# One product of 672 columns, cut along its rows, for the compressed queries, keys and rotary columns of the second mixer

## The reference

```python
def second_block(x, g_norm, w_in, ...):
    h = rms_norm(x, g_norm[l])
    proj = h @ w_in[l]
    hy_in, z_hy, c_q, c_kv, k_rope, z_attn, gate_hy, gate_attn = jnp.split(proj, split_at, axis=-1)
    ...
    q = (rms_norm(c_q, g_cq[l]) @ w_uq[l]).reshape(B, L, MLA_HEADS, QK_DIM)
    kv = (rms_norm(c_kv, g_ckv[l]) @ w_ukv[l]).reshape(B, L, MLA_HEADS, QK_NOPE + V_DIM)
    k_r = jnp.broadcast_to(k_rope[:, :, None, :], (B, L, MLA_HEADS, QK_ROPE))
```

## Time and profile before

| | |
|---|---|
| median of 3 runs | 1084.29 us (1083.72 to 1084.83) |
| the profiled execution, own time | 1085.98 us |
| its span, first to last instruction | 1084.2 us |
| TensorE (PE) busy, matmuls | 1078.1 us, 99% |
| weight loads (PEld) busy | 1020.2 us, 94% |
| VectorE (DVE) busy | 793.9 us, 73% |
| ScalarE (ACT) busy | 592.2 us, 55% |
| granted TensorE clock, mean | 1.000 |
| DMA mean | 176 GB/s |

### The profile page before, as it was taken

The page is one execution under the profiler, slowest core; times in us unless marked ns, Lnnn a source line. Parts: engine busy times, 40 slices in busy tenths (PEclk is TensorE's granted clock), DMA queues, the critical chain, the costliest instruction groups (busy, mean ns, idle before and its releaser), DMA issues.

```text
span 1084.2 us, 21114 instructions
## 1 busy us (share of the span) xinstructions
PE 1078.1 (99%) x8588; PEld 1020.2 (94%) x8588; DVE 793.9 (73%) x1117; ACT 592.2 (55%) x842; POOL 0.2 (0%) x4
## 2 busy tenths in 40 slices
PE   9999999999999999999999999999999999999999
PEld 7999999999989999999999998999999799999998
DVE  5665657989999877778778555775655887997784
ACT  5544444578643345878446546444444576655461
POOL 0000000000000000000000000000000000000000
PEclk9999999999999999999999999999999999999999
DMA  8765555455443454444656533465555356543341
GB/s 343 289 220 205 184 183 210 151 204 192 160 156 118 142 190 157 156 164 148 206 169 240 195 116 118 147 233 193 193 187 200 117 177 214 175 156 117 118 155 40
DMA packets 29170, 190.71 MB, mean 176 GB/s; under 512 B 3656, under 2 KB 4457, under 8 KB 7274
## 3 DMA queue, kind: packets, MB, share of 16 engines
q1 hardware_dynamic: 26480, 182.53, 48.2%
q10 hardware_dynamic: 2618, 7.14, 2.0%
HBM read 188.61 MB, written 1.05 MB: 175 GB/s over the span
## 4 chain that ended last, share of the span: by engine, by line
PE 96%; DVE 1%; DMA 1%; ACT 1%; issue 0%; SPq 0%; ACTq 0%; DVEq 0%
PE bank L525 16%; PE bank L526 16%; PE bank L527 16%; PE bank L537 11%; PE bank L538 11%; PE bank L539 11%; PE bank L624 3%; PE bank L760 1%; DMA sb_w_raw<-in_w 1%; PE bank L708 1%; PE bank L874 1%; PE bank L1022 1%; PE bank L1242 1%; PE bank L1034 1%; PE bank L1078 1%; PE bank L1100 1%
## 5 line engine op out<-in xcount | busy, mean ns | idle before, releaser
L2087 DVE TENSOR_TENSOR sb_w_lo<-sb_w_raw,sb_w_hi 128x2048 fp32r<-128x2048 f32 x169 | 386.4, 2289 | 129.6 <-ACT sb_w_hi L1370 128.9
L1370 ACT ACTIVATE sb_w_hi<-sb_w_raw 128x2048 fp32r<-128x2048 f32 x169 | 322.8, 1910 | 32.1 <-PE bank L527 27.9
L525 PE MATMUL bank<-sb_hT_hi,sb_w_hi 128*128 128x256 f32 (+1 forms) x816 | 226.0, 277 | 0.0
L527 PE MATMUL bank<-sb_hT_hi,sb_w_lo 128*128 128x256 f32 (+1 forms) x816 | 225.9, 277 | 0.0
L526 PE MATMUL bank<-sb_hT_lo,sb_w_hi 128*128 128x256 f32 (+1 forms) x816 | 225.8, 277 | 0.0
L537 PE MATMUL bank<-sb_hT_hi,sb_w_hi 128*128 128x256 f32 (+2 forms) x744 | 213.1, 286 | 0.0
L538 PE MATMUL bank<-sb_hT_lo,sb_w_hi 128*128 128x256 f32 (+2 forms) x744 | 206.4, 277 | 0.0
L539 PE MATMUL bank<-sb_hT_hi,sb_w_lo 128*128 128x256 f32 x744 | 206.1, 277 | 0.0
L525 PEld LDWEIGHTS bank<-sb_hT_hi,sb_w_hi 128*128 128x128 f32 (+1 forms) x816 | 152.8, 187 | 0.0
L526 PEld LDWEIGHTS bank<-sb_hT_lo,sb_w_hi 128*128 128x128 f32 (+1 forms) x816 | 152.7, 187 | 0.0
L527 PEld LDWEIGHTS bank<-sb_hT_hi,sb_w_lo 128*128 128x128 f32 (+1 forms) x816 | 152.7, 187 | 0.1
(11 more groups left out here) (513 smaller groups left out, 2092.7 us busy)
## 6 DMA issues: line engine op xcount, KB each, us to landing
sb_w_raw<-in_w SPq DMA_DIRECT2D x169, 1024.0 KB, 4.9
sb_w_raw<-in_w SPq DMA_DIRECT2D x4, 512.0 KB, 7.4
sb_hT<-in_xT SPq DMA_DIRECT2D x2, 512.0 KB, 5.3
sb_x<-in_x SPq DMA_DIRECT2D x2, 512.0 KB, 11.3
sb_mem_xn<-in_mem ACTq DMA_DIRECT2D x1, 1024.0 KB, 6.9
sb_mem_T<-in_memT ACTq DMA_DIRECT2D x1, 1024.0 KB, 10.4
sb_post_g<-in_ffn_post_g ACTq DMA_DIRECT2D x2, 512.0 KB, 5.8
sb_decay<-in_c_decay ACTq DMA_DIRECT2D x1, 768.0 KB, 5.4
```

The source lines that it names most:

```text
L525: pe.matmul(o, a_hi, b_hi, start=first, stop=False)
L527: return pe.matmul(o, a_lo, b_hi, start=False, stop=last)
L1370: act.activation(w_hi[b % STAGES][:], w_raw[b % RING][:], ACT.Copy).then_inc(w_hi_in, 1)
L2087: tt(w_lo[b % STAGES][:], w_raw[b % RING][:], f32(w_hi[b % STAGES][:]), ALU.subtract).then_inc(w_lo_in, 1)
```

## The change

The three blocks of c are cut in another way. Before, each held all 1024 rows and some of the columns: 256, 256 and 160. Now each holds all 672 columns and some of the rows: tiles k 0 to 2, 3 to 5, and 6 and 7 (`C_PARTS`). One block is used for 2 halves of the tokens and 2 halves of the columns, 336 each, so that four banks (0, 1, 2 and 7) are open at once and stay open over all three blocks; they can be read only when block 141 has been used. ScalarE therefore reads c after all three, in 8 instructions where there were 8 of other widths, and no longer between the roundings of blocks 142 and 143. `norm_turn(6)` still stands ahead of the third block, now in the middle of open sums. `zz0` takes bank 6, since bank 1 is not read by then. The entries of `WIDER` for `cq0` and `ckv` go.

```diff
--- before.py
+++ after.py
@@ -66,6 +66,10 @@
 
 W_IN_AT = {"q": 0, "k": 1024, "v": 2048, "z": 3072, "xbc": 5120, "dt": 8192, "gate": 8224}
 W_IN2_AT = {"hy": 0, "z_hy": 1536, "cq": 2048, "ckv": 2432, "rope": 2688, "z_at": 2720, "gate": 3232}
+
+
+C_PARTS = ((0, 3), (3, 3), (6, 2))
+C_WIDTH = Q_LORA + KV_LORA + QK_ROPE
 
 
 def weight_blocks():
@@ -100,9 +104,8 @@
     plain("xa_q", "xa_w_q", 0, 4)
     plain("xa_o", "xa_w_o", 0, 4)
     ffn(2)
-    add("cq", "w_in_2", [(W_IN2_AT["cq"], 256)])
-    add("ckv", "w_in_2", [(W_IN2_AT["ckv"], 256)])
-    add("cq_rope", "w_in_2", [(W_IN2_AT["cq"] + 256, P), (W_IN2_AT["rope"], QK_ROPE)])
+    for first, kt in C_PARTS:
+        add("c", "w_in_2", [(W_IN2_AT["cq"], C_WIDTH)], kt, first * P)
     plain("z_hy", "w_in_2", W_IN2_AT["z_hy"], 2)
     plain("z_at", "w_in_2", W_IN2_AT["z_at"], 2)
     add("uq", "w_uq_2", [(0, 512)], 3)
@@ -178,10 +181,10 @@
 
 WIDER = {**dict.fromkeys(("xbc1", "xbc10", "xbc11", "qkv1", "gate0", "gate2", "gate3", "gate4", "ssd5", "attn3.0", "zz3", "gg6",
                           "gg7", "hyo1.0", "qkv2", "qkv4", "qkv5", "hy0", "gg0", "gg3", "zz1"), (2, 2)),
-         **dict.fromkeys(("qkv7", "qkv3", "ssd7", "kv3", "kv6", "cq0", "gg2"), (4, 4)),
+         **dict.fromkeys(("qkv7", "qkv3", "ssd7", "kv3", "kv6", "gg2"), (4, 4)),
          **dict.fromkeys(("gate6", "hy4"), (8, 8)),
          **dict.fromkeys(("xo2", "qkv10", "z3"), (6, 0)),
-         "ckv": (4, 0), "qkv9": (2, 0), "qkv8": (12, 0), "z1": (10, 0), "out2": (12, 0)}
+         "qkv9": (2, 0), "qkv8": (12, 0), "z1": (10, 0), "out2": (12, 0)}
 
 
 
@@ -1134,18 +1137,39 @@
             for i in (6, 7):
                 filter_taps(i, (up + 2) % 3 if i == 6 else (up + 1) % 3)
             ffn_part(2, 4)
-            at = (0, 1, 2, 7, (FIRST["cq"] + 1) % 3, (FIRST["cq"] + 2) % 3)
+            at = (0, 1, 2, 7, (FIRST["c"] + 1) % 3, (FIRST["c"] + 2) % 3)
             for i in range(6):
                 filter_spectrum(i, at[i])
             raw_turn(5, x_added(3))
             for i in (6, 7):
                 filter_spectrum(i, at[i - 2])
-            token_block("cq0", FIRST["cq"], 256, sec_hi, sec_lo, ready=norm_done(5))
-            token_block("ckv", FIRST["ckv"], 256, sec_hi, sec_lo)
+            c_half, c_ready = C_WIDTH // 2, norm_done(5)
+            last_c = FIRST["c"] + len(C_PARTS) - 1
+
+            def c_block(i):
+
+                first, kt = C_PARTS[i]
+                hi, lo = weights(FIRST["c"] + i, kt, C_WIDTH)
+                for t in range(TOK):
+                    for h in range(2):
+                        key = f"c{t}.{h}"
+                        o = claim(key, (0, 1, 2, 7)[2 * t + h], last_c) if i == 0 else banks[fills[key][0]]
+                        for kk in range(kt):
+                            k = first + kk
+                            if t == 0 and h == 0:
+                                c_ready(k)
+                            a, w = slice(t * P, (t + 1) * P), slice(h * c_half, (h + 1) * c_half)
+                            mm = product(o[:, 0:c_half], sec_hi[:, k, a], sec_lo[:, k, a], hi[:, kk, w], lo[:, kk, w],
+                                         k == 0, k == KD - 1)
+                mm.then_inc(block_done, 1)
+
+            c_block(0)
+            c_block(1)
             norm_turn(6, sec_xn, 2)
-            token_block("cq1", FIRST["cq_rope"], P + QK_ROPE, sec_hi, sec_lo)
+            c_block(2)
             for i in range(4):
-                feature_block(f"zz{i}", FIRST["z_hy"] + i, 2, hT_hi, hT_lo, ready=None if i else norm_done(6))
+                feature_block(f"zz{i}", FIRST["z_hy"] + i, 2, hT_hi, hT_lo, bank=None if i else 6,
+                              ready=None if i else norm_done(6))
                 if i == 2:
 
                     pe.wait_ge(S("c_ready"), 4)
@@ -1882,31 +1906,28 @@
             act.dma_start(dft_a[:].rearrange("p w f -> p (w f)"), a["c_dft"][:, 0:512]).then_inc(S("dft_ab_in"), 16)
             act.dma_start(m_ropeT[:], a["c_rope"]).then_inc(S("rope_in"), 16)
 
-            def token_scale(dst, src):
-
-                for t in range(TOK):
-                    ins = act.activation(dst[:, t], src[:, t], ACT.Copy, scale=xr[:, t:t + 1])
-                return ins
-
-            o = full(act, "cq0")
-            act.wait_ge(S("xn_ready"), 3)
-            read(token_scale(cq[:, :, 0:256], two(o)), "cq0")
-            after(FIRST["cq"])
-            o = full(act, "ckv")
-            read(token_scale(ckv, two(o)), "ckv")
-            after(FIRST["ckv"])
+            after(FIRST["c"])
+            after(FIRST["c"] + 1)
             norm_high(6, "g_norm_2", hT_hi)
             act.dma_start(dft_b[:].rearrange("p w s -> p (w s)"), a["c_dft"][:, 1024:1536]).then_inc(S("dft_ab_in"), 16)
-            o = full(act, "cq1")
-            token_scale(cq[:, :, 256:384], two(o)[:, :, 0:P]).then_inc(S("cq1_in"), 1)
-            read(token_scale(k_rope, two(o)[:, :, P:P + QK_ROPE]), "cq1")
+            act.wait_ge(S("xn_ready"), 3)
+            mid = C_WIDTH // 2
+            for t in range(TOK):
+                r = xr[:, t:t + 1]
+                o = full(act, f"c{t}.0")
+                read(act.activation(cq[:, t, 0:mid], o[:, 0:mid], ACT.Copy, scale=r), f"c{t}.0")
+                o = full(act, f"c{t}.1")
+                n = Q_LORA - mid
+                act.activation(cq[:, t, mid:], o[:, 0:n], ACT.Copy, scale=r).then_inc(S("c_in"), 1)
+                act.activation(ckv[:, t], o[:, n:n + KV_LORA], ACT.Copy, scale=r).then_inc(S("c_in"), 1)
+                read(act.activation(k_rope[:, t], o[:, n + KV_LORA:mid], ACT.Copy, scale=r), f"c{t}.1")
 
             for t in range(TOK):
                 if t == 0:
 
-                    wait_read(act, "cq0")
-                    wait_read(act, "ckv")
-                    act.wait_ge(S("cq1_in"), 1)
+                    wait_read(act, "c0.0")
+                    wait_read(act, "c1.0")
+                    act.wait_ge(S("c_in"), 4)
                 else:
                     act.wait_ge(S("c_ssq"), 2)
                 act.activation(c_junk[:, 0:Q_LORA], cq[:, t, :], ACT.Square, accum_out=c_ssq[:, 0, t:t + 1])\
@@ -1914,7 +1935,7 @@
                 act.wait_ge(S("c_ssq"), 2 * t + 1)
                 act.activation(c_junk[:, 0:KV_LORA], ckv[:, t, :], ACT.Square, accum_out=c_ssq[:, 1, t:t + 1])\
                     .then_inc(S("c_ssq"), 1)
-            after(FIRST["cq_rope"])
+            after(FIRST["c"] + 2)
             for i in range(4):
                 o = full(act, f"zz{i}")
                 read(act.activation((z_hy if i < 2 else z_at)[:, 2 * (i % 2):2 * (i % 2) + 2, :], two(o), ACT.Silu), f"zz{i}")
@@ -2731,9 +2752,9 @@
             row_squares(x, sec_xn)
             row_root(5, xr[:])
             row_scale(x, sec_xn, xr)
-            low_after(FIRST["cq"])
+            low_after(FIRST["c"])
             norm_low(6, "g_norm_2", hT_hi, hT_lo)
-            low_after(FIRST["ckv"])
+            low_after(FIRST["c"] + 1)
 
 
             dve.wait_ge(S("c_ssq"), 4)
@@ -2756,7 +2777,8 @@
                 ins = stt(lo, o[:, k % 2 * SEQ:(k % 2 + 1) * SEQ], g, f32(hi), ALU.mult, ALU.subtract)
                 if k % 2 or k == 4:
                     read(ins, f"cT{k // 2}")
-            wait_read(dve, "cq1")
+            for t in range(TOK):
+                wait_read(dve, f"c{t}.1")
             for t in range(TOK):
                 ins = dve.tensor_copy(mq[:, 1, t, :, QK_NOPE:],
                                       k_rope[:, t, :].unsqueeze(1).to_broadcast([P, MLA_HEADS, QK_ROPE]))
```

## The result

The changed kernel takes 1086.44 us (median of 20 runs, 1084.93 to 1088.02), the kernel before 1084.73 (20 runs, 1083.66 to 1087.40): ratio 1.0015, 95% interval 1.0009 to 1.0021, so 1.0 to 2.3 us slower. I had forecast +1.06 us with a range of +0.4 to +1.9 of its own. It is slower by more than the noise, by about 0.15%.

A forecast was written before the change was run, and what follows sets the result against it. TensorE was taken as the bound. The product gives 2.2 us, the wait at bank 0 takes 1.8, the rest goes in the waits ahead of zz0 and zz2: +1.06 us, 1085.4 us, range +0.4 to +1.9 (1084.7 to 1086.2).

The forecast's parts named there:

- The wait for bank 0: First product of c waits until ScalarE has read the last spectrum from that bank: starts at 868.49, 1.78 us lost.
- The products: Matmuls of c: 16.67 us removed, 96 of 336 columns at 151 ns added, 14.50 us; 2.2 us less.
- zz0: First block after c, held by the last hT_lo read of bank 6: waits 0.83 us, starts 0.43 us later than before.
- The reads of c: ScalarE's eight reads, now all behind the last product: 2.31 us, from 884.90 to 887.21, making the squares 1.06 us later.
- zz2: Block held by block 144 from VectorE: starts at 897.11, 1.06 us later; TensorE itself waits 0.63 us.
- the shift stays: After zz2: everything hangs on zz2 or on VectorE, both equally late, so the 1.06 us remains to the end.
- a rival that needed the change to cause it: Blocks after zz1 change pace through a new phase: slower, +2.3 us, 1086.6 us (9%); faster, -0.1, 1084.2 us (6%).
- The kept gain: Rival: bank 0 free when TensorE comes, c starts at 866.71, sums of squares 0.72 us earlier; 1083.6 us (10%).
- The clock: Rival: TensorE's standing still at bank 0 and later brings the lower 1.2 GHz level; +3.5 us, 1087.8 us (8%).

The follow-up runs named there:

- e1: Changed kernel with the four banks of c in the order 1, 2, 0, 7 instead of 0, 1, 2, 7; 1084.66 us, ratio to the kernel before 0.9994.
- e2: Changed kernel with zz0 in bank 3 instead of bank 6; 1086.19 us, ratio to the kernel before 1.0009.
- e3: Changed kernel with ScalarE rounding block 144 before the squares and VectorE making its low part before the inverse roots; 1085.95 us, ratio to the kernel before 1.0010.
- e4: Changed kernel with the edits of e2 and e3 together; 1084.56 us, ratio to the kernel before 0.9992.
- e5: Changed kernel with its 672 columns cut at 384 instead of 336, so 6 reads of c, not 8; 1085.69 us, ratio to the kernel before 1.0009.
- e6: Changed kernel with the edits of e1, e2, e3 and e5 together; 1083.12 us, ratio to the kernel before 0.9987.
- e8: e6 plus ScalarE's and VectorE's work on the transposed c put ahead of block 147; 1082.03 us, ratio to the kernel before 0.9982.

## Why the prediction was right, and where it was off

**The wait for bank 0** was right in place and size: the first product 3.54 us after the spectra, forecast 3.50 (868.49 less 864.99). e1 takes it out and gets 1.90 us back. Not in my sum: the first matmul behind a wait takes 0.23 us to the second (869.33 to 869.56), 0.08 more than its width asks for, and the first behind the transposes 0.24 (882.17 to 882.41).

**The products** are the step that was mis-sized. I took 151 ns for 336 columns, between 149.8 and 154.6. In the first two blocks they take 154.2 (71 steps in the 10.95 us from 869.56 to 880.51); the row for the same stationary operand, `cq0`, would have given nearly that, 154.6, and I chose the 512 columns instead. That is 3.2 ns on 96, 0.31 us. The Trainium skill, page "TensorE: Matmul & The Clock Gate", section on the back-to-back issue gap, has N/2.4 + 2.5 ns for isolated matmuls, an estimate of 142.5 for this width. Measured are 12 ns more; the trace does not agree with it for these operands. The true saving of the product is 16.67 less 96 x 154.2 ns = 14.80, so 1.87 us for 2.2. That the load of the next weights sets the 111.7 ns of 160 columns was a guess of mine that no run tested; the sum used only the measured 111.7.

**`zz0`**: late by 0.87 us against the forecast 0.43, the late end of c (20.01 for 19.56) carried on, and by the mechanism named, the last `hT_lo`. e2 shows what the prediction implied: this wait stands in the shadow of the next.

**The reads of c**: 2.38 us for 2.31, from 20.42 for 19.91 after the spectra. **`zz2`**: late by 1.61 us for 1.06, held by block 144, released 0.05 us after it. e3, e4 and e5 each touch one link of that chain, and `zz2` moves as the chain says: 0.71, 1.57, 0.41. The statement that waits don't add up is shown by e4.

**What came after** is where the forecast said "the shift stays". In this pair of profiles it went from 1.61 at `zz2` to 1.43 at `uq0` and 1.25 at the end, because `zz2` and one later block ran in the quicker pace in the changed kernel's profile, 0.18 us each (`zz3` did too, but `uq0` is held by VectorE in both, so that gave nothing). With the second profiles it is 2.40 at the end (217.28 less 214.88). I had this as a rival that needed the change to cause it; the runs show that later blocks change pace from one execution to the next of one program, so that these differences need no change to explain them. They don't show that the program has no part in it: `zz0` and `zz1` were slow in e6 and e8 alone. The 1.71 us between the medians of 20 runs agree with the 1.61 at `zz2`, and, with an interval of 1.0 to 2.3, with the forecast 1.06 too; that 1.61 is the better number rests on the marks.

**The rivals.** The kept gain didn't come about; e1, which lets it in, gives 1.90 us back for my 1.78, and 0.29 us net gain at `zz2` for my 0.72, for the most part by the mis-sized width (0.31). The clock did not fall. The granted clock is 1.00 from 860 to 912 us, but that alone says little: it is listed as 1.00 too over the 26 matmuls at the start, so the lower level that I named there is read from their pace alone. What counts is the pace, and matmuls of 336 columns go at 154 ns right behind the wait.

## What to carry to other kernels

When narrow blocks are put together so that fewer and wider matmuls remain, look at what else the narrow cut gave: banks that come free one after the other, and reads that lie under the next block. Here 1.87 us of matmul time were saved and some 3.5 us added at `zz2` (the net shift of 1.61 and the 1.87), by the choice of two banks, the cut of the reads and the place of one block in two queues; none of it lies in the product, and with these four put right (e6) the change gains 1.3 parts in a thousand instead of losing 1.5. Take waits away along the chain, from its end: a wait in the shadow of a later one gives nothing until the later is gone.

## What was not expected of the hardware

The same program runs its matmuls of 256 columns at 113 or at 118 ns, block by block, at a granted clock of 1.00, and for many blocks differently in two executions: 1.34 us between two profiles of the kernel before. Others kept theirs: the 256 columns of `cq0` and `ckv` went at 118 ns in all three profiles that have them. What sets the pace stays open, and so does whether the slow `zz0` and `zz1` of e6 and e8, 0.37 us, come from the edits. The DMA share doesn't tell the two paces apart: `zz1` goes at 114 ns in e4 with a share of 0.86 (891.80 to 897.27), and at 118 ns in e6 with 0.84 (888.73 to 894.39). Two matmuls of 340 columns at the head of c left its 154 ns as they were. Besides, the last two spectra start anywhere between 863.64 and 866.17 us in the 13 profiles, though nothing ahead of them differs. Both together are why a microsecond needs 20 runs, while two marks in one trace show hundredths.
